# Embedding gates of a transformer kernel: the shifted order of tile m, chunk m-1 and chunk m-2, with sigmoid and product in a PSUM bank

## The chip, the cores and the metric

The kernel runs on one core of a Trainium2 chip. The metric is device time in microseconds (us) of one execution; lower is better. The engines are TensorE (PE, with its weight loads shown as PEld), VectorE (DVE), ScalarE (ACT), GpSimd (POOL) and SyncE (SP), which issues the weight DMAs. PSUM, the accumulation memory, has 8 banks of 128 x 512 f32.

## The reference

The model is two transformer layers (differential attention, then windowed attention, each followed by a convolutional FFN) and a third block, for 512 positions and width 1024. The change touches the last step of the first two layers, the gated embedding:

```
gate = jax.nn.sigmoid(rms_norm(h, ple_norm[i]) @ ple_w_gate[i])
h = h + (p[i] @ ple_w_proj[i]) * gate
return rms_norm(h, final_norm)          # after the last layer
```

The step is followed by an RMS norm and a projection: that of the attention of layer 1 after layer 0, and that of the third block after layer 1.

## The kernel before

The activations stand transposed, as 8 chunks `X[:, m, :]` of 128 features by 512 positions. Weights come as slabs of 128 x 1024 f32, one for an output tile. Every product is done in three matmuls of high and low parts (`hi*hi + hi*lo + lo*hi`), so a tile of 8 input chunks is 24 matmuls of 512 columns.

- A slab `s` is loaded by SP into one of 2 buffers `raw`, once POOL has finished slab `s - 2`. ACT copies it to `whi` (L981, function `used`, which first waits for the tile that last used this of the 4 places in the ring: slab s - 4). POOL writes `wlo = raw - whi` in two halves (L487), and PE waits for that. So the order in which ACT reaches its calls of `used` sets when PE gets weights.
- An input chunk `m` of the next stage is ready when ACT has written `Bhi` (L1002, `square_and_high`, which also writes the square `sq`, L1007) and DVE has written `Blo` (L1468, `low`). DVE adds the square into `acc` (L1475, `add_square`) for the norm.
- The normalisation is applied behind the matmul: `scaled` (L1459) multiplies the tile from PSUM by the row factor `R`, writes it to SBUF and frees the bank.

All engines run their instructions in the written order. In the stage `gate` there are 8 tiles. For each tile m, DVE does `scaled(m)`, adds the square of chunk m-1, waits for the sigmoid of ACT (L1245), multiplies by the projected embedding `pp` (L1765, into the SBUF buffer `gu`), adds to `X` (L1767) and waits for `Bhi` of the same chunk to write `Blo`. ACT does sigmoid(m), waits for the addition to `X`, writes `Bhi` and `sq`, and only then calls `used` for tile m, except for tiles 0 and 1. PE computes tiles 0 and 1 together, then 2 to 7 in order; tile m+4 needs the slab that ACT copies when it passes `used` of tile m, and so do the slabs of the stage behind. That stage is `kq2a` (two tiles, taken chunk by chunk) in layer 0 and `a3` (three tiles, each over chunks 0 to 6 first) in layer 1.

Lines: L495 matmuls, L981 `whi`, L487 `wlo`, L1459 `scaled`, L1245 sigmoid, L1765 product, L1767 addition, L1002 `Bhi`, L1007 `sq`, L1468 `Blo`, L1475 `acc`, L1511 the addition `X<-X,PS` of other stages.

Of the kernel before, what the change touches and what calls it, by code (L numbers as in the profile page):

```python
# [29 lines left out]
ALU = mybir.AluOpType  # L30
ACT = mybir.ActivationFunctionType
# [9 lines left out]
KC = D // P  # L41
# [127 lines left out]
def slab_of(stage, i, j):  # L169

    s = SLAB0[stage] + j
    return s + 4 * i, s % RING, s // RAWS + (4 // RAWS) * i
# [7 lines left out]
def tile_of(stage, i, j):  # L180

    banks = STAGE_BANKS.get(stage, (0, 1, 2, 3))
    bank = banks[j % len(banks)]
    earlier = sum(banks[t % len(banks)] == bank for t in range(j))
    return bank, BEFORE[stage][bank] + earlier + i


def build(nc, xT, pT, posd, wts, par, con, lamd, outT):
    ctx = ExitStack()
    with ctx:  # L190
        def sb(name, shape, dt=F32):
            return ctx.enter_context(nc.sbuf_tensor(name, shape, dt))

        def sem(name):
            return ctx.enter_context(nc.semaphore(name))
# [4 lines left out]
        X = sb("X", [P, KC, T])  # L200
# [37 lines left out]
        PS = ctx.enter_context(nc.psum_tensor("PS", [P, 8, T], F32))  # L238

        def chunks(b):  # L240
            return b[:, :].rearrange("p (k t) -> p k t", k=KC)

        def ar(off, n=1):
            v = AR[:, off:off + n * T]
            return v.rearrange("p (n t) -> p n t", n=n)
# [5 lines left out]
        def gain(name, col, m):  # L251
            if name == "both":
                return gfm[:, bass.ds(m, 1)]
            return par_sb[:, bass.ds(PCOLS[name][0] + col + m, 1)]
# [5 lines left out]
        def f32(a):  # L260
            return a.bitcast(F32)
# [15 lines left out]
        gt, gu, pp = ar(0, 2), ar(1024, 2), ar(4096, 8)  # L277
# [38 lines left out]
        sig_ready = sem("sig_ready")  # L316
        sdiff_ready, sink_ready = sem("sdiff_ready"), sem("sink_ready")
        ple_added = sem("ple_added")
# [656 lines left out]
        def _(act):  # L975
            own = Own(act, act_step)

            def high(s, slot, half):

                act.wait_ge(raw_ready[slot % RAWS], 16 * half + 16)  # L980
                act.activation(whi[:, slot, :], raw[:, slot % RAWS, :], ACT.Copy)\  # L981
                   .then_inc(hi_ready, 1)

            def used(stage, i, j, more=True):

                s, slot, half = slab_of(stage, i, j)
                act.wait_ge(slab_done, s + 1)
                if more:
                    high(s + RING, slot, half + RING // RAWS)

            def freed(stage, i, j):

                bank, before = tile_of(stage, i, j)
                act.wait_ge(tile_free[bank], before + 2)

            def square_and_high(norm, m, slot):

                n = NORMS.index(norm)
                c = KC * n + m
                if norm in GAIN:  # L1000
                    name, col = GAIN[norm]
                    act.activation(chunks(Bhi[BUF[norm]])[:, m, :], X[:, m, :], ACT.Copy,  # L1002
                                   scale=gain(name, col, m)).then_inc(xhi_ready, 1)
                if not (n == 0 and m < 2):

                    act.wait_ge(sq_used, c - 1)
                act.activation(sq[:, slot, :], X[:, m, :], ACT.Square).then_inc(sq_ready, 1)  # L1007

            def root(norm):
                n = NORMS.index(norm)  # L1010

                act.wait_ge(ss_done, n + 1)
                act.activation(rootc[:, :], PS[:, 7, 0:TB], ACT.Sqrt, scale=1.0 / D, bias=eps[:, 0:1])\
                   .then_inc(root_ready, 1)

            def rounds(n, body):
                if n == 1:
                    body(0)
                elif n == 2:
                    body(0)  # L1020
                    body(1)
                else:
                    with act.Fori(0, n) as i:
                        body(i)
# [203 lines left out]
            def embedding(l, nxt):  # L1228
                for q in range(2):
                    used(f"pp{l}", 0, q)  # L1230
                    for m in range(4):
                        bank, _ = tile_of(f"pp{l}", 0, 4 * q + m)
                        act.activation(pp[:, 4 * q + m, :], PS[:, bank, :], ACT.Copy)\
                           .then_inc(tile_free[bank], 1)
                root(f"ple{l}")

                act.wait_ge(r_ready, NORMS.index(nxt))

                def body(i):
                    for j in range(4):  # L1240
                        m = 4 * i + j
                        if m < 2:
                            used(f"gate{l}", i, j)
                        freed(f"gate{l}", i, j)
                        act.activation(gt[:, j % 2, :], gt[:, j % 2, :], ACT.Sigmoid)\  # L1245
                           .then_inc(sig_ready, 1)

                        act.wait_ge(ple_added, KC * l + m + 1)
                        square_and_high(nxt, m, j % 2)
                        if m >= 2:  # L1250
                            used(f"gate{l}", i, j)
                rounds(2, body)

            def split_p(l):
                act.wait_ge(p_in, 16 * l + 16)
# [192 lines left out]
        def _(dve):  # L1448
            own = Own(dve, dve_step)
            tt, stt, ts = dve.tensor_tensor, dve.scalar_tensor_tensor, dve.tensor_scalar  # L1450

            def done(stage, i, j):

                dve.wait_ge(slab_done, slab_of(stage, i, j)[0] + 1)

            def scaled(out, stage, i, j):

                bank, _ = tile_of(stage, i, j)
                tt(out, PS[:, bank, :], R[:, :], ALU.mult).then_inc(tile_free[bank], 1)  # L1459

            def low(norm, m):

                if norm in GAIN:
                    name, col = GAIN[norm]
                    k = KC * SPLITS.index(norm) + m
                    dve.wait_ge(xhi_ready, k + 1)
                    b = BUF[norm]
                    stt(chunks(Blo[b])[:, m, :], X[:, m, :], gain(name, col, m),  # L1468
                        f32(chunks(Bhi[b])[:, m, :]), ALU.mult, ALU.subtract).then_inc(x_split, 1)

            def add_square(norm, m, slot):
                c = KC * NORMS.index(norm) + m

                dve.wait_ge(sq_ready, c + 1)
                tt(acc[:, :], acc[:, :], sq[:, slot, :], ALU.add).then_inc(sq_used, 1)  # L1475
                dve.wait_ge(sq_used, c + 1)

            def low_and_add(norm, m, slot):
                low(norm, m)
                add_square(norm, m, slot)  # L1480

            def clear_sum():
                own.step(dve.memset(acc[:, :], 0.0))
                own.wait()

            def factor(norm):

                n = NORMS.index(norm)
                dve.wait_ge(root_ready, n + 1)
                dve.reciprocal(rcol[:, :], rootc[:, :]).then_inc(rcol_ready, 1)  # L1490
                dve.wait_ge(rspread, n + 1)
                dve.tensor_copy(R[:, :], PS[:, 7, :]).then_inc(r_ready, 1)
                dve.wait_ge(r_ready, n + 1)

            def rounds(n, per, body):
                if n <= 2:
                    for i in range(n):
                        body(i)
                else:
                    own.rounds(0, n, per, body)  # L1500
# [251 lines left out]
            def embedding(l, nxt):  # L1752
                factor(f"ple{l}")
                clear_sum()

                def body(i):
                    for j in range(4):
                        m = 4 * i + j
                        done(f"gate{l}", i, j)
                        scaled(gt[:, j % 2, :], f"gate{l}", i, j)  # L1760
                        if m:
                            add_square(nxt, m - 1, (j - 1) % 2)

                        dve.wait_ge(sig_ready, KC * l + m + 1)
                        own.step(tt(gu[:, j % 2, :], gt[:, j % 2, :], pp[:, m, :], ALU.mult))  # L1765
                        own.wait()
                        tt(X[:, m, :], X[:, m, :], gu[:, j % 2, :], ALU.add).then_inc(ple_added, 1)  # L1767
                        dve.wait_ge(ple_added, KC * l + m + 1)
                        low(nxt, m)
                rounds(2, 0, body)  # L1770
                add_square(nxt, KC - 1, (KC - 1) % 2)


            for b in range(BANKS):
# [87 lines left out]
            residual("o1", "ffn0")  # L1862
            feed_forward(0)
            embedding(0, "attn1")


# [20 lines left out]
            for m in range(KC):  # L1887
                c = KC * NORMS.index("mix") + m
# [365 lines left out]
```

## Time and profile before

| | |
|---|---|
| median of 3 runs | 2230.02 us (2226.22 to 2235.31) |
| the profiled execution | 2232.72 us, of which its span 2230.9 us |
| mean granted TensorE clock | 0.966 |
| PE busy | 2104.1 us (94%), 9896 matmuls |
| DVE busy | 1256.2 us (56%) |
| ACT busy | 977.8 us (44%) |
| POOL busy | 915.1 us (41%) |
| 16 sigmoids of the gates (L1245) | 630 to 633 ns each, from 735.2 to 1454.6 us |

The times in the rows below are microseconds from the start of the span. Layer 0's gate stage lies near 716 to 781 us, layer 1's near 1395 to 1460 us.

### The profile page before, as it was taken

What the parts mean: (1) busy time and instruction counts of PE and PEld (TensorE: products, weight loads), DVE (VectorE), ACT (ScalarE), POOL (GpSimd) and SP (SyncE); (2) the same over time, 40 slices, a digit from 0 to 9 for tenths busy, and PEclk for the clock granted to TensorE, in tenths of its full rate; (3) what the DMA queues carried; (4) which work ended last, traced back from release to release, by engine and by line L of the source; (5) the groups of instructions that cost most, each with busy time, mean ns of one, the idle gap of its engine ahead of it and who ended that gap; (6) DMA issues with size and microseconds to landing.
All of it is one profiled execution on the core that took longest, in us unless ns stands there. A gap on an engine that the chain in (4) does not pass through costs nothing. (4 is left out here: it accounts for less than half of the span.)

```text
span 2230.9 us, 28606 instructions
## 1 busy us (share of the span) xinstructions
PE 2104.1 (94%) x9896; PEld 1711.7 (77%) x9896; DVE 1256.2 (56%) x1830; ACT 977.8 (44%) x1547; POOL 915.1 (41%) x660
## 2 busy tenths in 40 slices
PE   6899899999999889899999999998979999999999
PEld 5677568888887667778888887777768778888887
DVE  5377756736265657866726356539688755213222
ACT  4577634524244456644524244434553334422222
POOL 4322034545455431124545455344104445445444
PEclk9899899999999989999999999999889999999999
DMA  3211012332323120012322323122102223322233
GB/s 139 76 48 48 29 57 94 96 102 94 99 94 110 62 71 29 30 38 89 109 95 94 104 94 114 57 95 67 39 19 76 85 76 97 102 95 95 99 99 104
DMA packets 49923, 179.53 MB, mean 80 GB/s; under 512 B 5536, under 2 KB 5792, under 8 KB 49824
## 3 DMA queue, kind: packets, MB, share of 16 engines
q1 hardware_dynamic: 48384, 174.09, 23.5%
q10 hardware_dynamic: 1440, 4.08, 0.5%
q8 instruction: 68, 1.11, 0.2%
q14 instruction: 31, 0.25, 0.0%
HBM read 176.05 MB, written 2.10 MB: 80 GB/s over the span
## 5 line engine op out<-in xcount | busy, mean ns | idle before, releaser
L487 POOL TENSOR_TENSOR wlo<-raw,whi 128x512 fp32r<-128x512 f32 x656 | 914.9, 1417 | 1301.3 <-ACT whi L981 1300.1
L495 PE MATMUL PS<-Bhi,whi 128*128 128x512 f32 x2368 | 942.2, 398 | 48.5 <-POOL wlo L487 25.8
L495 PE MATMUL PS<-Blo,whi 128*128 128x512 f32 x2368 | 931.5, 393 | 0.0
L495 PE MATMUL PS<-Bhi,wlo 128*128 128x512 f32 x2368 | 930.5, 393 | 0.0
L981 ACT ACTIVATE whi<-raw 128x1024 fp32r<-128x1024 f32 x328 | 345.5, 1056 | 598.8 <-PE PS L495 511.0
L495 PEld LDWEIGHTS PS<-Bhi,whi 128*128 128x128 f32 x2368 | 450.1, 190 | 162.7 <-issue 37.1
L495 PEld LDWEIGHTS PS<-Bhi,wlo 128*128 128x128 f32 x2368 | 450.2, 190 | 96.0
L495 PEld LDWEIGHTS PS<-Blo,whi 128*128 128x128 f32 x2368 | 450.3, 190 | 91.5 <-issue 0.5
L1459 DVE TENSOR_TENSOR AR<-PS,R 128x512 f32<-128x512 f32 x172 | 116.6, 689 | 223.3 <-PE PS L495 212.0
L1511 DVE TENSOR_TENSOR X<-X,PS 128x512 f32<-128x512 f32 x96 | 65.8, 687 | 231.6 <-PE PS L495 230.6
L1719 DVE SCALAR_TENSOR_TENSOR AR<-AR,par_sb 128x511 f32<-128x511 f32 x88 | 117.5, 1336 | 8.8 <-ACT AR L1205 8.8
L1931 DVE SCALAR_TENSOR_TENSOR AR<-AR,par_sb 128x512 f32<-128x512 f32 x120 | 116.8, 1030 | 0.0
L1220 ACT ACTIVATE Bhi<-AR 128x512 f32 x66 | 41.8, 633 | 167.0 <-DVE AR L1735 167.0
L1722 DVE SCALAR_TENSOR_TENSOR AR<-AR,par_sb 128x511 f32<-128x511 f32 x88 | 106.8, 1213 | 12.9 <-DVE AR L1719 2.9
L1096 ACT ACTIVATE AR<-PS,nmax 128x512 f32<-128x512 f32 (+3 forms) x160 | 93.3, 590 | 42.2 <-DVE nmax L1583 40.3
L1468 DVE SCALAR_TENSOR_TENSOR Blo<-X,par_sb,Bhi 128x512 fp32r<-128x512 f32 x56 | 63.6, 1136 | 46.8 <-ACT Bhi L1002 46.6
L1117 ACT ACTIVATE pthi<-PS 128x512 fp32r<-128x512 f32 (+3 forms) x128 | 56.7, 477 | 74.0 <-PE PS L718 72.9
L1205 ACT ACTIVATE AR<-AR,par_sb 128x512 f32<-128x512 f32 x88 | 70.9, 806 | 37.5 <-DVE AR L1459 37.5
L1739 DVE TENSOR_TENSOR Blo<-AR,Bhi 128x512 f32 x66 | 47.1, 714 | 61.5 <-ACT Bhi L1220 61.5
L1475 DVE TENSOR_TENSOR acc<-acc,sq 128x512 f32<-128x512 f32 x64 | 77.5, 1211 | 0.0
L718 PE MATMUL PS<-constR,AR 128*128 128x128 f32 x368 | 61.7, 300 | 16.1 <-DVE ptlo L1632 13.1
L495 PE MATMUL PS<-qkhi 64*128 64x512 f32 (+3 forms) x160 | 48.9, 482 | 29.3 <-ACT AR L1096 20.4
(222 smaller groups left out, 2111.1 us busy)
## 6 DMA issues: line engine op xcount, KB each, us to landing
raw<-in_weights SPq DMA_DIRECT2D x328, 512.0 KB, 3.2
X<-in_xT ACTq DMA_DIRECT2D x4, 512.0 KB, 7.7
out<-X SPq DMA_DIRECT2D x8, 256.0 KB, 3.2
AR<-in_pT ACTq DMA_DIRECT2D x2, 512.0 KB, 4.2
par_sb<-in_parameters ACTq DMA_DIRECT2D x1, 322.0 KB, 4.5
AR<-in_positions ACTq DMA_DIRECT2D x1, 256.0 KB, 9.1
con_sb<-in_constants ACTq DMA_DIRECT2D x1, 206.5 KB, 8.9
AR<-in_lambdas ACTq DMA_DIRECT2D x1, 128.0 KB, 8.9
```

What stands on the lines that cost most here:

```text
L487: ins = pool.tensor_tensor(wlo[:, j, c], raw[:, j % RAWS, c], f32(whi[:, j, c]), ALU.subtract)
L495: return pe.matmul(out, w, x, start=start, stop=stop)
L981: act.activation(whi[:, slot, :], raw[:, slot % RAWS, :], ACT.Copy)\
L1096: act.activation(probs(kind)[:, 2 * (g % 2) + s, 0:nb * P], PS[:, score_bank(kind, n), 0:nb * P], ACT.Exp, bias=nmax[:, n % 4:n % 4 + 1], ...
L1205: act.activation(cv[:, 2 * pair + u, :], us[:, 2 * pair + u, :], ACT.Identity, scale=conv_w[:, l, 1, u, bass.ds(q, 1)], bias=conv_w[:, l, ...
L1459: tt(out, PS[:, bank, :], R[:, :], ALU.mult).then_inc(tile_free[bank], 1)
L1468: stt(chunks(Blo[b])[:, m, :], X[:, m, :], gain(name, col, m), f32(chunks(Bhi[b])[:, m, :]), ALU.mult, ALU.subtract).then_inc(x_split, 1)
L1475: tt(acc[:, :], acc[:, :], sq[:, slot, :], ALU.add).then_inc(sq_used, 1)
L1511: tt(X[:, m, :], X[:, m, :], PS[:, bank, :], ALU.add)\
L1719: own.step(stt(c[:, 1:T], x[:, 0:T - 1], conv_w[:, l, 0, u, bass.ds(q, 1)], c[:, 1:T], ALU.mult, ALU.add))
L1722: stt(c[:, 0:T - 1], x[:, 1:T], conv_w[:, l, 2, u, bass.ds(q, 1)], c[:, 0:T - 1], ALU.mult, ALU.add).then_inc(conv_done, 1)
L1931: ins = stt(out, src, k, out, ALU.mult, ALU.add)
```

## The change

DVE now does in one round m: `scaled(m)`; product and addition of chunk m-1; `Blo` and square sum of chunk m-2. ACT does in one round m: sigmoid(m), `used` of tile m, then `Bhi` and `sq` of chunk m-1. The sigmoid is written to PSUM bank 7 instead of in place, and the product is made in place in that bank; so DVE reads one SBUF operand in each of the two. As the bank is single, ACT waits before sigmoid(m) until the addition of chunk m-1 is done.

```diff
 (ACT, embedding)
-                def body(i):
-                    for j in range(4):
-                        m = 4 * i + j
-                        if m < 2:
-                            used(f"gate{l}", i, j)
-                        freed(f"gate{l}", i, j)
-                        act.activation(gt[:, j % 2, :], gt[:, j % 2, :], ACT.Sigmoid)\
-                           .then_inc(sig_ready, 1)
-
-                        act.wait_ge(ple_added, KC * l + m + 1)
-                        square_and_high(nxt, m, j % 2)
-                        if m >= 2:
-                            used(f"gate{l}", i, j)
-                rounds(2, body)
+                for m in range(KC + 1):
+                    if m < KC:
+                        freed(f"gate{l}", m // 4, m % 4)
+                        if m:
+
+                            act.wait_ge(ple_added, KC * l + m)
+                        act.activation(PS[:, 7, :], gt[:, m % 2, :], ACT.Sigmoid).then_inc(sig_ready, 1)
+                        used(f"gate{l}", m // 4, m % 4)
+                    if m:
+
+                        act.wait_ge(ple_added, KC * l + m)
+                        square_and_high(nxt, m - 1, (m - 1) % 2)
 (DVE, embedding)
-                        done(f"gate{l}", i, j)
-                        scaled(gt[:, j % 2, :], f"gate{l}", i, j)
-                        if m:
-                            add_square(nxt, m - 1, (j - 1) % 2)
-
-                        dve.wait_ge(sig_ready, KC * l + m + 1)
-                        own.step(tt(gu[:, j % 2, :], gt[:, j % 2, :], pp[:, m, :], ALU.mult))
+                for m in range(KC + 2):
+                    if m < KC:
+                        done(f"gate{l}", m // 4, m % 4)
+                        scaled(gt[:, m % 2, :], f"gate{l}", m // 4, m % 4)
+                    if 1 <= m <= KC:
+                        c = m - 1
+                        dve.wait_ge(sig_ready, KC * l + c + 1)
+                        own.step(tt(PS[:, 7, :], PS[:, 7, :], pp[:, c, :], ALU.mult))
                         own.wait()
-                        tt(X[:, m, :], X[:, m, :], gu[:, j % 2, :], ALU.add).then_inc(ple_added, 1)
-                        dve.wait_ge(ple_added, KC * l + m + 1)
-                        low(nxt, m)
-                rounds(2, 0, body)
-                add_square(nxt, KC - 1, (KC - 1) % 2)
+                        tt(X[:, c, :], X[:, c, :], PS[:, 7, :], ALU.add).then_inc(ple_added, 1)
+                    if m >= 2:
+                        dve.wait_ge(ple_added, KC * l + m - 1)
+                        low_and_add(nxt, m - 2, m % 2)
```

On ACT, at the start of layer 0's gates, the order before was (`AR` holds the gates, `raw`/`whi` are the weights):

```order
L981 ACTIVATE whi<-raw 128x1024 [waits raw_ready0,slab_done,r_ready]
L1245 ACT_TABLE_LOAD
L1245 ACTIVATE AR<-AR 128x512 [waits tile_free0]
L1002 ACTIVATE Bhi<-X,par_sb 128x512 [waits ple_added]
L1007 ACTIVATE sq<-X 128x512 [waits sq_used]
L981 ACTIVATE whi<-raw 128x1024 [waits raw_ready1,slab_done]
L1245 ACTIVATE AR<-AR 128x512 [waits tile_free1]
L1002 ACTIVATE Bhi<-X,par_sb 128x512 [waits ple_added]
L1007 ACTIVATE sq<-X 128x512 [waits sq_used]
L1245 ACTIVATE AR<-AR 128x512 [waits tile_free2]
```

In the same place it is now:

```order
L1245 ACT_TABLE_LOAD [waits tile_free0]
L1245 ACTIVATE PS<-AR 128x512 [waits r_ready]
L981 ACTIVATE whi<-raw 128x1024 [waits raw_ready0,slab_done]
L1245 ACTIVATE PS<-AR 128x512 [waits ple_added,tile_free1]
L981 ACTIVATE whi<-raw 128x1024 [waits raw_ready1,slab_done]
L1002 ACTIVATE Bhi<-X,par_sb 128x512 [waits ple_added]
L1007 ACTIVATE sq<-X 128x512 [waits sq_used]
L1245 ACTIVATE PS<-AR 128x512 [waits ple_added,tile_free2]
L981 ACTIVATE whi<-raw 128x1024 [waits raw_ready0,slab_done]
```

The first copy of weights moved behind the table load and the first sigmoid; every later one moved ahead of `Bhi` and `sq` of its round.

On DVE, a round of the gates in layer 0 was before (`Blo` and `acc` belong to the next norm; AR<-PS,R is `scaled`):

```order
L1459 TENSOR_TENSOR AR<-PS,R 128x512 [waits slab_done]
L1475 TENSOR_TENSOR acc<-acc,sq 128x512 [waits sq_ready]
L1765 TENSOR_TENSOR AR<-AR 128x512 [waits sig_ready,sq_used]
L1767 TENSOR_TENSOR X<-X,AR 128x512 [waits dve_step]
L1468 SCALAR_TENSOR_TENSOR Blo<-X,par_sb,Bhi 128x512 [waits xhi_ready,ple_added]
```

A round is now, with the line numbers of the changed kernel:

```order
L1457 TENSOR_TENSOR AR<-PS,R 128x512 [waits slab_done,sq_used]
L1761 TENSOR_TENSOR PS<-PS,AR 128x512 [waits sig_ready]
L1763 TENSOR_TENSOR X<-X,PS 128x512 [waits dve_step]
L1466 SCALAR_TENSOR_TENSOR Blo<-X,par_sb,Bhi 128x512 [waits xhi_ready,ple_added]
L1473 TENSOR_TENSOR acc<-acc,sq 128x512 [waits sq_ready]
```

The five instructions are the same in number; they now belong to three different chunks, and the product and the addition read and write PSUM. PE's order is unchanged.

## Rows read from the trace of the kernel before

**Rows 1.** Waits, 707 to 830 us: engine waited for: us total, times, longest.

```profile
ACT Bhi L1002 <- DVE X L1767: 23.6, 8, 3.4
```

**Rows 2.** Timeline of PE, layer 0: start, duration, engine, instruction, [idle before <-releaser].

```profile
740.10 0.39 PE L495 MATMUL PS<-Bhi,whi 128*128 128x512 f32 x1
...
750.76 0.39 PE L495 MATMUL PS<-Bhi,wlo 128*128 128x512 f32 x1
754.04 0.50 PE L495 MATMUL PS<-Bhi,whi 128*128 128x512 f32 x1 [2.89 <-POOL wlo L487]
...
767.13 0.40 PE L495 MATMUL PS<-Bhi,wlo 128*128 128x512 f32 x1
772.60 0.80 PE L495 MATMUL PS<-Bhi,whi 128*128 128x512 f32 x1 [5.07 <-POOL wlo L487]
...
779.01 0.40 PE L495 MATMUL PS<-Bhi,whi 128*128 128x512 f32 x1
```

**Rows 3.** Stretch of PE: length, busy (instructions), granted clock, DMA share, GB/s.

```profile
754.00:759.00 5.00, 4.96 (x15) 0.66 0.32 105
```

**Rows 4.** Timeline of POOL, layer 0.

```profile
733.97 2.53 POOL L487 TENSOR_TENSOR wlo<-raw,whi 128x512 fp32r<-128x512 f32 x2 [15.60 <-ACT whi L981]
...
756.84 3.35 POOL L487 TENSOR_TENSOR wlo<-raw,whi 128x512 fp32r<-128x512 f32 x2 [2.86 <-ACT whi L981]
763.04 3.35 POOL L487 TENSOR_TENSOR wlo<-raw,whi 128x512 fp32r<-128x512 f32 x2 [2.85 <-ACT whi L981]
```

**Rows 5.** Timeline of ACT, one round of layer 0.

```profile
760.77 0.72 ACT L1002 ACTIVATE Bhi<-X,par_sb 128x512 fp32r<-128x512 f32 x1 [3.36 <-DVE X L1767]
...
761.92 1.04 ACT L981 ACTIVATE whi<-raw 128x1024 fp32r<-128x1024 f32 x1
762.98 0.63 ACT L1245 ACTIVATE AR<-AR 128x512 f32<-128x512 f32 x1
```

**Rows 6.** Timeline of DVE, one round of layer 0.

```profile
755.39 0.75 DVE L1468 SCALAR_TENSOR_TENSOR Blo<-X,par_sb,Bhi 128x512 fp32r<-128x512 f32 x1 [0.86 <-ACT Bhi L1002]
756.06 0.68 DVE L1459 TENSOR_TENSOR AR<-PS,R 128x512 f32<-128x512 f32 x1
756.66 0.68 DVE L1475 TENSOR_TENSOR acc<-acc,sq 128x512 f32<-128x512 f32 x1
757.51 1.52 DVE L1765 TENSOR_TENSOR AR<-AR 128x512 f32<-128x512 f32 x1 [0.17 <-ACT AR L1245]
759.06 1.67 DVE L1767 TENSOR_TENSOR X<-X,AR 128x512 f32<-128x512 f32 x1
```

**Rows 7.** Instructions of two lines: count, ns min/median/max, first and last start.

```profile
L1459 DVE TENSOR_TENSOR AR<-PS,R x172: 675/692/694, 354.1 to 2195.2; 128x512 f32<-128x512 f32 x172
...
L1511 DVE TENSOR_TENSOR X<-X,PS x96: 679/687/691, 307.9 to 2227.8; 128x512 f32<-128x512 f32 x96
```

**Rows 8.** Timelines of DVE and ACT, start of layer 0's gates.

```profile
733.49 0.69 DVE L1459 TENSOR_TENSOR AR<-PS,R 128x512 f32<-128x512 f32 x1
...
733.91 1.28 ACT L1245 ACT_TABLE_LOAD   x1
```

**Rows 9.** Timelines of ACT and POOL behind `kq2a`.

```profile
791.14 1.06 ACT L981 ACTIVATE whi<-raw 128x1024 fp32r<-128x1024 f32 x1 [9.63 <-PE PS L495]
...
792.27 5.05 POOL L487 TENSOR_TENSOR wlo<-raw,whi 128x512 fp32r<-128x512 f32 x4 [8.16 <-ACT whi L981]
...
798.19 1.06 ACT L981 ACTIVATE whi<-raw 128x1024 fp32r<-128x1024 f32 x1 [3.46 <-DMA raw<-in_weights]
```

**Rows 10.** Timeline of PE, layer 1.

```profile
1429.99 0.39 PE L495 MATMUL PS<-Bhi,wlo 128*128 128x512 f32 x1
...
1454.02 0.50 PE L495 MATMUL PS<-Bhi,whi 128*128 128x512 f32 x1 [3.85 <-DVE Blo L1468]
...
1457.96 0.44 PE L495 MATMUL PS<-Blo,whi 128*128 128x512 f32 x1
```

**Rows 11.** Attention of layer 1: length, busy of PE, PEld, DVE, ACT, POOL; clock, DMA, GB/s.

```profile
812.00:823.00 11.00, 3.82 (x21) 3.08 (x21) 6.18 (x12) 8.77 (x15) 4.99 (x4) 0.54 0.21 63
```

More of the change, by code:

```diff
@@ L1754, in embedding @@
                 clear_sum()
-                def body(i):
-                    for j in range(4):
-                        m = 4 * i + j
-                        done(f"gate{l}", i, j)
-                        scaled(gt[:, j % 2, :], f"gate{l}", i, j)
-                        if m:
-                            add_square(nxt, m - 1, (j - 1) % 2)
-                        dve.wait_ge(sig_ready, KC * l + m + 1)
-                        own.step(tt(gu[:, j % 2, :], gt[:, j % 2, :], pp[:, m, :], ALU.mult))
-                        own.wait()
-                        tt(X[:, m, :], X[:, m, :], gu[:, j % 2, :], ALU.add).then_inc(ple_added, 1)
-                        dve.wait_ge(ple_added, KC * l + m + 1)
-                        low(nxt, m)
-                rounds(2, 0, body)
-                add_square(nxt, KC - 1, (KC - 1) % 2)
+                for m in range(KC + 2):
[6 more added lines that the diff above has]
+                        own.step(tt(PS[:, 7, :], PS[:, 7, :], pp[:, c, :], ALU.mult))
+                        own.wait()
+                        tt(X[:, c, :], X[:, c, :], PS[:, 7, :], ALU.add).then_inc(ple_added, 1)
+                    if m >= 2:
+                        dve.wait_ge(ple_added, KC * l + m - 1)
+                        low_and_add(nxt, m - 2, m % 2)
             for b in range(BANKS):
```

## The prediction, made before the changed kernel was run

> **What bounds the kernel now.** I read the page first: PE is busy for 94% of the span, so a change pays only where PE stands still or runs at its lower clock. Then I listed the waits of the stretch around layer 0's gates. The largest entry that the change touches is ACT in front of `Bhi`, waiting for DVE's addition: 23.6 us in 8 times [rows 1]. That is no wait of PE, so I read the timelines of this stretch engine by engine.
>
> PE [rows 2]: in the steady parts one matmul starts 0.227 us after the last (740.10 to 750.76 is 47 steps), so a tile of 24 takes 5.44 us. Tile 6 starts at 754.04 and not at 750.99; the second tile of `kq2a` starts at 772.60, though the first three matmuls of that stage were over at 767.5. PE waits for POOL's `wlo` in both places, 2.89 and 5.07 us. Behind the first wait the granted clock averages 0.66 over 5 us, so for part of them it is at the lower of its two levels, 1.2 GHz and not 2.4 [rows 3]; behind the second, 15 steps take 6.41 us (772.60 to 779.01), nearly twice their time.
>
> Both waits are for weights, and the weights come once in 6.20 us: POOL's starts are 756.84 and 763.04 [rows 4]. POOL is idle for 2.85 us between them, waiting for ACT. ACT copies `whi` only behind `sq` of the same chunk, and stands 3.36 us in front of `Bhi` [rows 5]. What it waits for is DVE. There a round is closed: `Blo`, `scaled`, `acc`, product 1.52, addition 1.67, and behind it 0.86 us of waiting for `Bhi` [rows 6]; start to start (0.67, 0.60, 0.85, 1.55, 1.67 and the wait) that is the same 6.2 us. So DVE and ACT hand each chunk to and fro, this ring takes 6.2 us where PE needs 5.44, and through `used` it sets PE's weights. In layer 1 the second wait has another cause, the input chunk itself (`Blo` of chunk 6), 3.85 us [rows 10].
>
> Two parts of the ring are long for what they do. Product and addition run from 757.51 to 760.73, POOL from 756.84 to 760.19, and POOL's pair takes 3.35 us there against 2.53 us [rows 4, 6]. Instructions of DVE with one PSUM operand never show this: the 172 of `scaled` and the 96 of L1511 are at most 694 and 691 ns [rows 7].
>
> **The change part by part.**
>
> *Product and addition with PSUM.* The addition `X<-X,PS` has the form of L1511: 0.69 us, and it saves 0.98 us a chunk. The product reads and writes PSUM, a form of which the trace has no row. Nearest rows: `scaled`, 0.69 us with PSUM on one side; from above the 1.52 us of today's product. I take 0.69. The sigmoid to PSUM has no row either: 0.63 us today [rows 5]; my bounds are 0.31 and 1.26, half and twice that, and I take 0.63.
>
> *The new round.* DVE start to start: `scaled` 0.60, product 0.72, addition 0.62 to 0.7, `Blo` 0.67, `acc` with its wait 0.85: 3.5 us. ACT: sigmoid 0.63, `whi` 1.04, `Bhi` 0.63, `sq` 0.6: 2.9 us. The ring that is left is sigmoid(m), which waits for addition(m-1), and product(m), which waits for sigmoid(m). Nothing in it waits for `Bhi`, as `Blo` is two chunks behind. Both sums are below PE's 5.44, so PE sets the pace, and DVE waits for it at `scaled`. Let G be the end of a gate tile. Then `scaled` runs at G+0.1, product at G+0.8, addition to G+2.2, sigmoid from G+2.35, `whi` from G+3.0, POOL from G+4.1 to G+6.7. DVE's two instructions with two SBUF operands, `Blo` and `acc`, are over at G+3.7, so POOL should need its 2.53. The weights for the tile four on are ready at G+6.7; PE wants them at G+16.3. With the product at its upper bound a round of DVE is 4.3 us, with the sigmoid at its own one of ACT is 3.5, both still below 5.44: these two unknowns cost PE nothing in the steady state.
>
> *The first rounds.* The first `whi` now stands behind the table load and sigmoid(0), and the load waits for `scaled`(0). From [rows 8]: 734.18 + 0.15, load to 735.6, sigmoid to 736.25, `whi` to 737.2, `wlo` to 739.85. PE wants it at 740.10 [rows 2]. It was there at 736.50, so the cover of 3.6 us shrinks to 0.25; I charge 0.15 us a layer (0 to 0.8, the upper end if POOL takes 3.3). Behind it the two raw buffers hold ACT up, because SP starts slab s only when POOL has finished s-2. From POOL's 794.8 (the second of four pieces) to ACT's 798.19 is 3.4 us [rows 9]. So `whi` of the slab for tile 6 starts at 743.3 and not right behind sigmoid(2), and `wlo` is ready at about 747 to 748; for tile 7 at 750; for the two tiles of `kq2a` at 755 and 758. PE wants them at 751.0, 756.4 and twice at 761.9. ACT's queue behind such a DMA wait holds `Bhi` and the next sigmoid, and DVE is late by about 1 us at tile 4, but by tile 6 (G = 756.8) it waits for PE again.
>
> By the Trainium skill, page "ScalarE: Activation LUTs", section "Rules for kernel authors" (the row on a tight latency budget), a change of function set should be budgeted at about 2.7 us; this trace has 1.28 [rows 8]. With 2.7 the first `wlo` would be 1.4 us later, PE would stand 1.2 us in both layers, and the sum below would be 2.1 us smaller. The row is of this very load, so I go by it.
>
> *Layer 0.* PE runs without a wait from 750.99: 48 matmuls of tiles 6 and 7 and three of `kq2a` are 51 x 0.2267 = 11.56, so the matmul that started at 772.60 starts at 762.55: 10.05 us. The chunks keep up: chunk 6 is wanted at 770.0 and its `Blo` is done 5.8 to 6.5 us behind the end of tile 7 (762.05), at 767.9 to 768.6. The lower clock goes with the waits: 6.41 - 15 x 0.2267 = 3.01 us. Together 13.06 us.
>
> *Layer 1.* Tiles 6 and 7 end at 1441.25 (1429.99 + 48 x 0.2267 + 0.39). Behind this: `scaled`(7) 1441.4, product(6) 1442.0, addition(6) to 1443.4, `Blo` and `acc` of chunk 5 to 1444.7, product(7) 1444.9, addition(7) to 1446.3, `Blo`(6) to 1447.0, or 1447.8 if POOL, which is at work from 1445.25, is in its way. PE wants chunk 6 after 18 matmuls of `a3`, at 1445.2. So a wait of 1.8 to 2.6 us stays, and the matmul of 1454.02 starts at about 1447.4: 6.6 us. The lower clock behind the old wait, 1454.02 to 1457.96 for 10 steps, goes: 3.94 - 2.27 = 1.67 us [rows 10]. Together 8.3 us (6.2 to 8.6).
>
> *What is late next.* Nothing behind this that I see holds its time: the attention of layer 1 and the third block begin with PE's norm sum and with `used` of the first tile, and both move with PE. `sq` for the second norm of the third block is done by ACT and DVE alone and moves by more than PE does.
>
> **The sum.** 13.06 + 8.3 - 2 x 0.15 = 21.1 us. On the profiled execution: 2232.72 - 21.1 = 2211.6. That execution is 2.7 us above the median of the runs (2230.02, runs 2226.2 to 2235.3), so for a median I say 2230.0 - 21.1 = 2209 us.
>
> **The rivals.**
>
> *A. PE keeps part of its lower clock or a wait.* In the new order a wait of about 2.2 us is left in layer 1, and one can open at tile 4. For: the clock fell behind waits of 2.9 us and more. Against: the waits now are shorter than that. It would return 1.7 us in layer 1, 0.8 us twice at tile 4, up to 3 us if the clock falls there too, and the `Blo` behind POOL 0.8: gain 14 to 17, time about 2215.
>
> *B. The gain of layer 0 is lost in the attention behind it.* For: from 812 to 823 us PE is busy for 3.82 of 11 us and ACT for 8.77 [rows 11], and at 798.19 a weight DMA is waited for. Against: that DMA follows `wlo`, which follows `whi` at 791.14, and this waited 9.63 us for PE [rows 9]. If it held, only layer 1's 8.3 us are left: 2222 us.
>
> *C. Slower: the single bank as a ring.* Product and addition of chunk m-1, sigmoid(m) and product(m) are now strictly one behind another through bank 7, and DVE must write PSUM, which no row shows. The other three instructions of DVE take 2.1 us in a round; when product and addition together pass 3.3 us (1.35 today by my count) DVE is slower than PE, and from 4.1 us on slower than today's 6.2. At 3 us each a round is 8.1 us, 1.9 more than now, for about 7 rounds in both layers: +26 us, less the 5 us of lower clock if that no longer falls: 2250 us. For it speaks only that the form is not in the trace; against it the 268 instructions with PSUM at 0.69 [rows 7].
>
> **How the numbers follow.** My forecast 0.70 (own range 2204 to 2214: the bounds above and the spread of the runs), A 0.14, B 0.12, C 0.04. About 0.5%, 11 us, is what a measurement of this kernel can tell from no change. Forecast and A are beyond it, but for a tail of A of 0.01 or 0.02; B is within. So faster 0.83, same 0.13, slower 0.04. The range has to hold 8 in 10, and so reaches over A: 2203 to 2219.
>
> **What would show it.** In the changed profile the product and the addition should be at 0.69 us, POOL's pair near 2.5 us, starts of POOL's pairs 5.44 us apart late in the stage, and no PE wait for `wlo` between tile 4 and the end of `kq2a`; the granted clock should be 1.00 from layer 0's gates to the end of `kq2a`, and ACT's `whi` of 791.14 should start at about 778. In layer 1 one wait of PE of about 2 us for `Blo` should be left. A product above 1.5 us, a wait at tile 4 of more than 0.8 us, or that `whi` later than 781 would prove me wrong, and in this order by C, by the first rounds, and by A.

## The result and the profile after

The changed kernel takes 2210.43 us (2206.68 to 2211.95) against 2230.06 us for the kernel before, run beside it: ratio 0.990, 95% interval 0.989 to 0.992. Forecast were 2209 us and a range of 2203 to 2219. In a second group of runs it took 2209.36 us, against 2231.89 us for the kernel before: ratio 0.990 (0.988 to 0.992).

The profiled execution has a span of 2204.9 us, 26.0 less than before. The page's busy times, which answer to the table of before:

```profile
PE 2096.9 (95%) x9896; PEld 1709.7 (78%) x9896; DVE 1242.8 (56%) x1830; ACT 978.3 (44%) x1547; POOL 911.2 (41%) x660
```

To compare executions I use one measure: from the start of tile 2's first matmul to the norm sum behind `kq2a` (layer 0) and behind `a3` (layer 1), both read from PE's rows. Before it is 63.48 and 68.79 us, now 50.37 and 60.17: 21.7 us of the 26.0. Of the rest, some 3 us lie in the third block, which the change doesn't touch. They are spread between executions: in a second profiled one the measure is 50.38 and 60.17, but the span 2208.5, and the medians of the runs differ by 19.6 us.

PE in the two stages, before and after (length, busy and instructions, granted clock, DMA share, GB/s):

```profile
716.00:782.00 66.00, 57.69 (x240) 0.92 0.20 64
1407.00:1476.00 69.00, 62.26 (x265) 0.95 0.21 70
```

```profile
716.00:782.00 66.00, 66.00 (x338) 1.00 0.21 72
1397.00:1453.00 56.00, 54.31 (x241) 1.00 0.28 93
```

In the same 66 us PE now does 338 instructions and not 240 (some of them the shorter matmuls of the stage behind), with no wait and at the full clock. The waits of [rows 2] are gone. In layer 1 one is left, 1.69 us against 3.85 in [rows 10] (timeline of PE after):

```profile
1430.82 0.39 PE L495 MATMUL PS<-Bhi,wlo 128*128 128x512 f32 x1
1432.90 0.50 PE L495 MATMUL PS<-Bhi,whi 128*128 128x512 f32 x1 [1.69 <-DVE Blo L1466]
1433.24 0.40 PE L495 MATMUL PS<-Blo,whi 128*128 128x512 f32 x1
```

The matmuls behind it are 0.2 to 0.3 us apart, so the clock did not fall.

The edited instructions (count, ns min/median/max, first and last start), of which the trace of before had no product and no sigmoid in this form:

```profile
L1761 DVE TENSOR_TENSOR PS<-PS,AR x16: 689/691/700, 735.7 to 1430.6; 128x512 f32<-128x512 f32 x16
...
L1763 DVE TENSOR_TENSOR X<-X,PS x16: 686/689/690, 736.4 to 1431.3; 128x512 f32<-128x512 f32 x16
...
L1245 ACT ACTIVATE PS<-AR x16: 581/604/607, 735.1 to 1429.4; 128x512 f32<-128x512 f32 x16
```

That it was POOL which made product and addition long, the trace of before shows by itself. In one round of layer 0 POOL stands idle, from 743.44 to 750.69 us, and there both take 0.69 us; a round earlier POOL is at work, and they take 1.53 and 1.66 (DVE's timeline, then POOL's):

```profile
740.76 1.53 DVE L1765 TENSOR_TENSOR AR<-AR 128x512 f32<-128x512 f32 x1 [0.17 <-ACT AR L1245]
742.32 1.66 DVE L1767 TENSOR_TENSOR X<-X,AR 128x512 f32<-128x512 f32 x1
...
746.97 0.69 DVE L1765 TENSOR_TENSOR AR<-AR 128x512 f32<-128x512 f32 x1 [0.17 <-ACT AR L1245]
747.69 0.69 DVE L1767 TENSOR_TENSOR X<-X,AR 128x512 f32<-128x512 f32 x1
```

```profile
740.08 3.36 POOL L487 TENSOR_TENSOR wlo<-raw,whi 128x512 fp32r<-128x512 f32 x2 [3.58 <-ACT whi L981]
```

A round of DVE now, to be held against [rows 6]:

```profile
756.20 0.69 DVE L1457 TENSOR_TENSOR AR<-PS,R 128x512 f32<-128x512 f32 x1 [1.00 <-PE PS L495]
756.81 0.69 DVE L1761 TENSOR_TENSOR PS<-PS,AR 128x512 f32<-128x512 f32 x1
757.53 0.69 DVE L1763 TENSOR_TENSOR X<-X,PS 128x512 f32<-128x512 f32 x1
758.14 0.75 DVE L1466 SCALAR_TENSOR_TENSOR Blo<-X,par_sb,Bhi 128x512 fp32r<-128x512 f32 x1
758.80 0.68 DVE L1473 TENSOR_TENSOR acc<-acc,sq 128x512 f32<-128x512 f32 x1
761.64 0.69 DVE L1457 TENSOR_TENSOR AR<-PS,R 128x512 f32<-128x512 f32 x1 [2.15 <-PE PS L495]
```

DVE waits for PE, and the round is PE's 5.44 us. POOL's timeline (to [rows 4]) shows how it came there:

```profile
736.73 5.50 POOL L487 TENSOR_TENSOR wlo<-raw,whi 128x512 fp32r<-128x512 f32 x4 [18.86 <-ACT whi L981]
743.88 5.97 POOL L487 TENSOR_TENSOR wlo<-raw,whi 128x512 fp32r<-128x512 f32 x4 [1.65 <-ACT whi L981]
...
759.98 2.55 POOL L487 TENSOR_TENSOR wlo<-raw,whi 128x512 fp32r<-128x512 f32 x2 [2.36 <-ACT whi L981]
765.42 3.00 POOL L487 TENSOR_TENSOR wlo<-raw,whi 128x512 fp32r<-128x512 f32 x2 [2.89 <-ACT whi L981]
```

Late in the stage a pair takes 2.55 to 3.00 us. In the first rounds two pairs take 5.50 and 5.97, and `Blo` and `acc`, which still read two SBUF operands, are long where they meet POOL: 1.57 and 1.77 us at 739.52 and 741.01, against 0.75 and 0.68 above.

### The profile page after: what moved, and what is told of

Same layout as the page of the kernel before. It is cut to its first block and busy times, and to the rows that moved or that the text cites. A ratio compares the mean times of both kernels' runs of the same rounds, so it can differ in the third digit from the quotient of the medians.

```text
span 2204.9 us, 28620 instructions
## 1 busy us (share of the span) xinstructions
PE 2096.9 (95%) x9896; PEld 1709.7 (78%) x9896; DVE 1242.8 (56%) x1830; ACT 978.3 (44%) x1547; POOL 911.2 (41%) x660
## 5 line engine op out<-in xcount | busy, mean ns | idle before, releaser
L1473 DVE TENSOR_TENSOR acc<-acc,sq 128x512 f32<-128x512 f32 x64 | 85.2, 1331 | 0.0
```

## The experiments

The gate stage decides the time, so each run is read by its ratio to the kernel before and by the measure above. Waits and stretches are told in the same way as above. The change again and the next three kernels ran in one group, where the kernel before took 2231.89 us; the last four ran in another, where it took 2229.49. So between the groups ratios are compared, not times. The measure comes from one profiled execution of each kernel.

**The change again**, beside the first three experiments.

> The changed kernel as it is, as the measure for the other kernels of this group. By the traces of one execution each, 13.1 us come from layer 0 and 8.6 us from layer 1, 21.7 us together; the 4.3 us that the two profiled executions differ by beyond that lie before the gates and in the attention of the third block, which the change doesn't touch, and I take them for spread. So I expect 20 to 23.5 us less than before (ratio 0.9895 to 0.9910). If a further part of the change's effect is real outside the gate stages, the gain is 25 us or more.

2209.36 us (2208.17 to 2211.53), ratio 0.990 (0.988 to 0.992).

**Only the PSUM bank, in the order of before.** ACT's and DVE's loops are those of before, with three operands changed:

```diff
-                        act.activation(gt[:, j % 2, :], gt[:, j % 2, :], ACT.Sigmoid)\
+                        act.activation(PS[:, 7, :], gt[:, j % 2, :], ACT.Sigmoid)\
-                        own.step(tt(gu[:, j % 2, :], gt[:, j % 2, :], pp[:, m, :], ALU.mult))
+                        own.step(tt(PS[:, 7, :], PS[:, 7, :], pp[:, m, :], ALU.mult))
-                        tt(X[:, m, :], X[:, m, :], gu[:, j % 2, :], ALU.add).then_inc(ple_added, 1)
+                        tt(X[:, m, :], X[:, m, :], PS[:, 7, :], ALU.add).then_inc(ple_added, 1)
```

> The old order of both engines; only sigmoid and product are in PSUM bank 7. Theory 1 (one closed ring per chunk that has to be faster than PE's 5.44 us): the ring shrinks from 6.2 to 6.2 - 0.83 - 0.98 = 4.4 us, below 5.44, so PE sets the pace with the old order too. By the rows, copies of weights stay behind sq, round m of DVE starts at 733.0, 738.9, 743.3, 747.7 and so on; the second slab of kq2a is then ready at about 764, 1.5 us after PE wants it, so layer 0 gains about 11.5 us of its 13.1; in layer 1 chunk 6 is ready by the time PE wants it, so the 1.7 us wait that the changed kernel has there goes, and it gains about 10.4 us. Together 20 to 23 us, the same as the whole change within 2 us. Rival 2 (the shifted order is what matters, since it takes Bhi and Blo out of the ring): with the old order ACT and DVE still hand each chunk to and fro and less than 8 us is gained. Rival 3 (what matters is VectorE and GpSimd in each other's way): the full gain here, and next to none with the order alone.

2208.57 us (2207.36 to 2212.86), ratio 0.990 (0.988 to 0.992), measure 52.33 and 58.65: 21.3 of the 21.7 us, without the new order. DVE's timeline, one round:

```profile
754.55 0.75 DVE L1468 SCALAR_TENSOR_TENSOR Blo<-X,par_sb,Bhi 128x512 fp32r<-128x512 f32 x1 [0.86 <-ACT Bhi L1002]
...
756.64 0.70 DVE L1765 TENSOR_TENSOR PS<-PS,AR 128x512 f32<-128x512 f32 x1
757.37 0.69 DVE L1767 TENSOR_TENSOR X<-X,PS 128x512 f32<-128x512 f32 x1
758.92 0.75 DVE L1468 SCALAR_TENSOR_TENSOR Blo<-X,par_sb,Bhi 128x512 fp32r<-128x512 f32 x1 [0.86 <-ACT Bhi L1002]
```

The ring of before, with its wait of 0.86 us for `Bhi`, is still there, but it takes 4.37 us and not 6.2, less than PE's 5.44. What the old order costs in layer 0 is 2.0 us, of which one wait is 1.23 (PE):

```profile
763.30 0.50 PE L495 MATMUL PS<-Bhi,whi 128*128 128x512 f32 x1 [1.23 <-POOL wlo L487]
```

In layer 1 the old order is the better one by 1.5 us: it makes `Blo` of the same chunk in the round, not two rounds later, so chunk 6 is there when `a3` wants it, and PE's wait of 1.69 us is gone.

**Only the order, in SBUF.** With two SBUF buffers in place of the single bank, ACT's wait for the addition of the chunk before goes too.

```diff
-                        if m:
-
-                            act.wait_ge(ple_added, KC * l + m)
-                        act.activation(PS[:, 7, :], gt[:, m % 2, :], ACT.Sigmoid).then_inc(sig_ready, 1)
+                        act.activation(gt[:, m % 2, :], gt[:, m % 2, :], ACT.Sigmoid).then_inc(sig_ready, 1)
-                        own.step(tt(PS[:, 7, :], PS[:, 7, :], pp[:, c, :], ALU.mult))
+                        own.step(tt(gu[:, c % 2, :], gt[:, c % 2, :], pp[:, c, :], ALU.mult))
-                        tt(X[:, c, :], X[:, c, :], PS[:, 7, :], ALU.add).then_inc(ple_added, 1)
+                        tt(X[:, c, :], X[:, c, :], gu[:, c % 2, :], ALU.add).then_inc(ple_added, 1)
```

> The shifted order, with the sigmoid in place in SBUF and the product from SBUF to SBUF as before (two buffers, so ACT doesn't wait for the addition of the chunk before). Theory 1: a round of DVE has no wait in it and takes 3.5 us plus what GpSimd costs it, 1 to 2 us, so at most 5.44: PE sets the pace, layer 0 gains its 13.1 us. At the end of layer 1 the product of chunk 7 or the Blo of chunk 6 runs beside GpSimd and PE's wait for Blo grows from 1.7 to 2.5 to 3.5 us, perhaps with the lower clock behind it: 5 to 8 us there. Together 18 to 20.5 us, 1 to 3.5 us less than the whole change. Rival 2 (order): the same. Rival 3 (VectorE and GpSimd in each other's way is what made the ring slow): product and addition still take 1.5 and 1.7 us and less than 8 us is gained.

2224.15 us (2220.42 to 2225.93), ratio 0.996 (0.995 to 0.998), measure 53.66 and 68.08, 10.5 us below before: about half of the gain by the measure, a third by the medians. The expectation (18 to 20.5 us) missed. DVE's timeline:

```profile
759.69 0.69 DVE L1454 TENSOR_TENSOR AR<-PS,R 128x512 f32<-128x512 f32 x1
760.30 1.06 DVE L1758 TENSOR_TENSOR AR<-AR 128x512 f32<-128x512 f32 x1
761.40 0.69 DVE L1760 TENSOR_TENSOR X<-X,AR 128x512 f32<-128x512 f32 x1
762.00 0.74 DVE L1463 SCALAR_TENSOR_TENSOR Blo<-X,par_sb,Bhi 128x512 fp32r<-128x512 f32 x1
762.67 1.78 DVE L1470 TENSOR_TENSOR acc<-acc,sq 128x512 f32<-128x512 f32 x1
764.49 0.69 DVE L1454 TENSOR_TENSOR AR<-PS,R 128x512 f32<-128x512 f32 x1
```

The late rounds take 4.8 us, below 5.44, as I had expected. But DVE never waits for PE: `scaled` of tile 7 starts at 764.49, some 3 us behind the tile's end. In layer 0 PE then waits 2.41 us for `Blo`, besides 0.29 for the first `wlo`. In layer 1 it waits 2.39 and 3.09 us, each followed by matmuls at the lower clock, at 0.63 us and not 0.40 (PE's timeline, then a stretch at 1.2 GHz):

```profile
1436.73 0.79 PE L495 MATMUL PS<-Bhi,whi 128*128 128x512 f32 x1 [2.39 <-DVE Blo L1463]
1437.33 0.63 PE L495 MATMUL PS<-Blo,whi 128*128 128x512 f32 x1
...
1441.47 0.80 PE L495 MATMUL PS<-Bhi,whi 128*128 128x512 f32 x1 [3.09 <-DVE Blo L1463]
```

```profile
1438.00:1446.00 8.00, 4.91 (x12) 0.50 0.21 68
```

**Three pads of DVE in every round**, as a bound on what a slower product would do:

```diff
                         scaled(gt[:, m % 2, :], f"gate{l}", m // 4, m % 4)
+                        for _ in range(3):
+                            own.step(dve.memset(gu[:, 0, :], 0.0))
+                            own.wait()
```

> The changed kernel with three idle memsets (0.5 us each, to a buffer that nobody reads) behind scaled in each of the 8 rounds of each layer, so in front of the product. It adds 1.6 us of VectorE to a round, 5.1 us instead of 3.5. Theory 1: still below PE's 5.44, so layer 0 changes by nothing (0 to 0.5 us), and in layer 1 only the last round counts: the Blo of chunk 6 is 1.6 us later, PE's wait grows from 1.7 to 3.3 us, and as the clock fell behind 2.9 us before, another 1.7 us: 1.5 to 4 us slower than the changed kernel. If the ring through the single bank (product, addition, sigmoid, product) or the order were already at the limit, each of 7 rounds would be longer by up to 1.6 us and the kernel 10 to 20 us slower than the changed one.

2223.58 us (2221.14 to 2229.86), ratio 0.997 (0.995 to 0.998), measure 54.94 and 69.00: 14 us slower than the change, and another miss. DVE's timeline, first and last instruction of a round, and one pad:

```profile
761.80 0.69 DVE L1457 TENSOR_TENSOR AR<-PS,R 128x512 f32<-128x512 f32 x1
...
763.21 0.48 DVE L1759 MEMSET AR<- 128x512 f32 x1 [0.17 <-DVE AR L1759]
...
767.11 0.69 DVE L1457 TENSOR_TENSOR AR<-PS,R 128x512 f32<-128x512 f32 x1
```

A pad costs 0.66 us, the round takes 5.3 us: still below 5.44. Two misses of one kind made me form another theory. A round shorter than PE's is not enough. DVE begins the stage behind PE (in the change its first `scaled` is at 733.00, when PE is at the end of tile 2), and it makes up only the difference between 5.44 and its own round. With 5.3 that is next to nothing: here DVE is 5.2 us behind tile 4's end and still 4.8 behind tile 7's. What is left there becomes PE's wait in the next stage. The rival: a pad costs its own time wherever it stands. Half of the pads, once early and once late, tell these apart.

The expectation also named 10 to 20 us as the loss if the ring through the single bank were the limit, and 14 lies in that range. PE has no wait before the end of tile 7, so this ring doesn't make its tiles longer. But it has a part in the arrears: ACT waits 2.59 us for an addition before each late sigmoid, `used` stands behind the sigmoid, and so PE's first wait is for weights (timelines of ACT and PE):

```profile
760.60 0.60 ACT L1245 ACTIVATE PS<-AR 128x512 f32<-128x512 f32 x1 [2.59 <-DVE X L1766]
```

```profile
764.82 0.50 PE L495 MATMUL PS<-Bhi,whi 128*128 128x512 f32 x1 [1.78 <-POOL wlo L487]
...
765.67 0.63 PE L495 MATMUL PS<-Bhi,whi 128*128 128x512 f32 x1
```

What a second bank would save of this was not run.

**The pads in rounds 0 to 3, and in rounds 4 to 7.**

```diff
+                        for _ in range(3 if m < 4 else 0):
```

```diff
+                        for _ in range(3 if m >= 4 else 0):
```

> The changed kernel with the three memsets (2.0 us with their waits) only in rounds 0 to 3 of both layers. The kernel with them in all rounds was 14 us slower than the changed one where I had expected 1.5 to 4. Theory now (arrears): what decides is not whether a round of VectorE is shorter than PE's 5.44 us, but how late VectorE is when tile 7 ends; the first rounds leave it late, and each later round pays back only 5.44 minus its length. Unpadded rounds take 3.5 to 4.2 us and pay back 1.2 to 1.9 us each, so arrears from rounds 0 to 3 are nearly gone by tile 7: 0 to 2.5 us slower than the changed kernel, PE's wait for Blo in layer 1 between 1.7 and 3 us. Rival (each pad costs its own time wherever it stands, since VectorE's chain bounds the stage): half of the 14 us, about 7.

> The same four pads, in rounds 4 to 7. Theory of arrears: in the changed kernel VectorE waits 1.0 us at tile 6 and 2.2 us at tile 7; four pads of 1.7 to 2 us use that up and leave it about 2 us late at tile 7, and the pad of round 7 comes on top: Blo of chunk 6 is 3.5 to 4.5 us later. Layer 1: PE's wait for Blo grows from 1.7 to 5 or 6 us, with the lower clock behind it (1.7 us): 5 to 7 us. Layer 0: chunk 6 had about 2.7 us to spare there, so 0.5 to 2 us. Together 6 to 9 us slower than the changed kernel, and 4 to 8 us more than the early pads. Rival (each pad costs its own time wherever it stands): the same as the early pads, about 7 us.

Early: 2209.26 us (2206.33 to 2210.63), ratio 0.991 (0.989 to 0.992), measure 51.08 and 60.67, 1.2 us above the change. Late: 2213.03 us (2212.74 to 2213.49), ratio 0.993 (0.991 to 0.995), measure 51.91 and 65.86, 7.2 us above. The same 12 pads in each layer, six times the price by the measure, and 3.8 us apart by the medians. Both lie within what the theory of arrears had said (0 to 2.5 and 6 to 9 us); the rival had said about 7 for either. Starts of `scaled` for tiles 4 and 7 in layer 0, on DVE, with the pads early:

```profile
751.00 0.69 DVE L1457 TENSOR_TENSOR AR<-PS,R 128x512 f32<-128x512 f32 x1
...
763.78 0.69 DVE L1457 TENSOR_TENSOR AR<-PS,R 128x512 f32<-128x512 f32 x1
```

and with the pads late:

```profile
747.30 0.69 DVE L1457 TENSOR_TENSOR AR<-PS,R 128x512 f32<-128x512 f32 x1
...
763.22 0.69 DVE L1457 TENSOR_TENSOR AR<-PS,R 128x512 f32<-128x512 f32 x1
```

With early pads DVE is 5.2 us behind tile 4's end (745.8, by PE's start of tile 2 and 5.44 us a tile) and 1.6 us behind tile 7's (762.1): it has paid back some 3.5. With late pads it is 2.2 us behind tile 4 and 1.8 behind tile 7 and has paid back almost nothing. So at tile 7 both are about equally late in layer 0; what still differs is round 7, whose 2.0 us of pads lie behind PE's last tile, where nothing hides them. In layer 1 `Blo` of chunk 5 starts 35.9 us behind the start of the measure in the change, 36.4 with early pads and 39.7 with late ones. Of these 3.8 us, 2.0 are round 7's pads, the rest arrears. PE in layer 1, late pads (timeline, then a stretch):

```profile
1434.96 0.73 PE L495 MATMUL PS<-Bhi,whi 128*128 128x512 f32 x1 [3.26 <-DVE Blo L1466]
...
1437.87 0.79 PE L495 MATMUL PS<-Bhi,whi 128*128 128x512 f32 x1 [1.32 <-DVE Blo L1466]
```

```profile
1438.00:1442.00 4.00, 4.00 (x10) 0.51 0.39 131
```

The waits are 2.9 us more than the change's 1.69; the other 2.8 of the 5.7 us in this layer go for the most part with the lower clock behind them.

**The old order in layer 1, the new one in layer 0**, with PSUM in both (the loops of before under `else`):

```diff
+                if l == 0:
                     for m in range(KC + 1):
...
+                else:
+                    def body(i):
+                        for j in range(4):
...
+                            act.activation(PS[:, 7, :], gt[:, j % 2, :], ACT.Sigmoid)\
```

> Layer 0 in the shifted order, layer 1 in the old order, both with sigmoid and product in PSUM. By the stretches of the traces so far: layer 0 as in the changed kernel, 62.2 us from the first gate matmul to the norm sum of kq2a (75.3 before, 64.1 with the old order and PSUM); layer 1 as in the kernel with PSUM alone, 58.6 us from tile 2 to the norm sum behind a3 (68.8 before, 60.2 changed), no wait of PE for Blo. Together 23.2 us less than before, 1.5 less than the changed kernel, which is below what the runs can tell; the two stretches in the trace decide. If the two layers depended on each other (slabs or DMA carried over), one of the stretches would be longer by over 0.5 us.

2206.88 us (2205.25 to 2208.6), ratio 0.990 (0.988 to 0.992), measure 50.37 and 58.63: both stages at their best value so far, 1.5 us below the change, and PE has no wait at all from 1395 to 1470 us. By the medians alone this can't be told from the change.

**The first copy of weights ahead of the table load, as before.**

```diff
+                used(f"gate{l}", 0, 0)
...
-                        used(f"gate{l}", m // 4, m % 4)
+                        if m:
+                            used(f"gate{l}", m // 4, m % 4)
```

> The changed kernel with the first copy of weights back ahead of the table load and the first sigmoid. I had charged 0.15 us a layer for its place behind them. In the trace of the changed kernel PE has no wait at tile 4, so the time should be the same (within 0.5 us by the stretches, within the spread by the runs). What should move: wlo for tile 4 is done 2 to 3 us earlier, the third copy no longer waits 2.3 us for the weight DMA, and VectorE's arrears are smaller by 1 to 2 us. If the late first copy cost anything, layer 0's stretch of 62.2 us would be shorter by more than 0.5.

2209.74 us (2207.68 to 2211.97), ratio 0.992 (0.990 to 0.993), measure 50.37 and 60.18, equal to the change's. POOL's first `wlo` moves from 736.73 to 732.97 and gains nothing. DVE is in step earlier (it waits for PE already at tile 5), and that is worth nothing either, since in the change it is in step by tile 6:

```profile
750.26 0.69 DVE L1459 TENSOR_TENSOR AR<-PS,R 128x512 f32<-128x512 f32 x1 [0.95 <-PE PS L495]
```

## Why the prediction was right

- **What bounds the kernel**: right. A ring of 6.2 us set PE's weights; with 4.37 us (PSUM alone) PE waits for weights only once, 1.23 us, and with the ring cut as well (the change) never.
- **Product and addition in PSUM**: 0.69 forecast, 0.691 and 0.689 measured. The sigmoid was put at 0.63 and is 0.604.
- **Layer 0**: 13.06 us less 0.15, measured from the first gate matmul 13.11 (75.29 to 62.18). The first `wlo` cost PE nothing. The granted clock is 1.00 over the whole stretch, and ACT's `whi` of 791.14 [rows 9] starts at 777.54, where I had said 778.
- **Layer 1**: 8.3 us less 0.15, measured 8.62, of which 6.99 up to the start of the matmul of 1454.02 (forecast 6.6). The wait left is 1.69, just below my 1.8 to 2.6.
- **The first rounds**: the direction right, the size off. I had DVE about 1 us late at tile 4. It was 2.3 us late, as POOL, `Blo` and `acc` met there and POOL took 5.5 to 6.0 us for two pairs, where I had counted 2.53 each. It was back in step at tile 6, as I had said, and the error cost nothing. There was room for it: with the early pads DVE is 5.2 us late at tile 4, and that costs 1.2 us. But the prediction had not worked this room out.
- **Rivals A and B** didn't come about: no fall of the clock behind 1.69 us, and nothing lost behind `kq2a`.
- **Rival C** didn't either, but its point of decision was wrong. The prediction says that DVE is slower than PE only when product and addition together pass 3.3 us, and that either unknown at its upper bound costs PE nothing in the steady state. The pads lengthen this pair from 1.35 to about 3.3 us, the round stays at 5.3, and 14 us are lost. A bound on the steady state doesn't hold for 8 rounds in which DVE is behind from the start, with these pads 5.2 us at tile 4. (The 1.35 us that the prediction calls today's is its count for the new kernel; in the kernel before the pair takes 3.2.) Had the product taken its upper bound of 1.52, a round of 4.3 would have paid back 1.1 us each time, and my sum would have held roughly; that was not run.
- **What I had not separated**: I credited the gain to both edits. The PSUM operands bring nearly all of it, the order 2.0 us in layer 0 and minus 1.5 in layer 1 on top of them. Order alone gave 10.5 us, because the collisions with POOL stay: in the late rounds the product takes 1.06 us, `acc` 1.78 and the pair of POOL 3.5, where the change has 0.69, 0.68 and 2.55.

By the Trainium skill, page "SBUF — State Buffer", section "Who interferes with whom", a DVE instruction with two SBUF inputs contends with a GpSimd instruction that reads SBUF, and one with at most one SBUF input, outside the modes that use both ports, doesn't. These traces agree: with a PSUM operand all 32 of the edited instructions are at most 0.70 us, also those that run beside POOL from start to end; with two SBUF operands the 16 products of before are 0.69 to 1.53, and 0.69 only in the round of each layer in which POOL is idle.

## What to carry to other kernels

Where DVE and POOL work at once, look for DVE instructions of one shape whose duration varies twofold; giving one operand a place in PSUM made them constant here and shortened POOL's as well, and that was worth more than reordering the rounds. Compare a helper engine's round with PE's, but also count how late it is when the stage begins and how many rounds it has to make that up: time added early was nearly free here, the same time added late cost six times as much by the measure. An order that defers a step by two rounds suits a stage whose successor wants weights first, and not one whose successor wants the last chunk.

## What the runs showed of the hardware

- DVE reading and writing PSUM in one instruction (128x512 f32, the other input in SBUF) takes 0.69 us, as much as with PSUM on one side or, undisturbed, none. ACT's sigmoid is 28 ns shorter into PSUM (604 ns) than into SBUF (632).
- Two SBUF inputs beside POOL's work: product up to 1.65 us (in the order alone) for 0.69, addition 1.67 for 0.69, `acc` 1.79 for 0.68, `Blo` 1.78 for 0.75; POOL's pair 3.35 to 3.53 for 2.53.
- The granted clock stayed at 1.00 behind single waits of PE of 1.23 us (PSUM alone), 1.69 (the change), 1.76 (early pads) and 2.41 (order alone, layer 0). It was at the lower level behind 1.78 us (three pads, layer 0, where the matmuls from 765.67 on take 0.63 us), behind 2.39 in layer 1 of the order alone, and behind 3.09, 3.26 and 4.33. Waits of nearly the same length, 1.76 and 1.78, 2.41 and 2.39, are found on both sides, so the length alone doesn't decide; what does stays open.
